# Two sums of squares over partitions: one f32 product each, or two rounded products of a split square

## Chip, cores and metric

One NeuronCore of a Trainium2 chip runs the whole kernel in one launch. The metric is device time in microseconds (us). The engines are TensorE (PE, with its weight loads as PEld), VectorE (DVE), ScalarE (ACT), GpSimd (POOL) and SyncE (SP, which issues most DMAs). Each engine works through its own queue in order.

## What is computed

A decoder layer with two branches on x of 1024 x 1024 (f32). Cut to what matters here:

```
proj = h @ w_in[l]                                   # the large product
o_a = hgrn2_chunked(q, k_in, v, log_f)               # branch A, 4 heads of 128
o_a = rms_norm(o_a, hg_norm_gain) * silu(hg)
o_b = diff_attention(dq, dk, dv, lam)                # branch B, 4 heads of 128
o_b = rms_norm(o_b, diff_norm_gain) * (1 - lam_init) * silu(dg)
y = sigmoid(ma) * (o_a @ w_branch_a) + sigmoid(mb) * (o_b @ w_branch_b)
x = x + gate * rms_norm(y @ w_out, g_post)
```

`rms_norm` divides by the root of the mean of squares over the 128 values of a head. In the kernel a head's outputs lie with those 128 values on the 128 partitions and the 1024 positions along the free dimension, so that the mean is a sum over partitions.

## The kernel before

The input projection is done in rounds of 28 products (four groups of seven, a Strassen scheme: M1, M2, M6, M5, M7, M3, M4). A product is 12 matmuls of 128x128 by 128x512 in the rounded type fp32r (each operand split into a high and a low part; lines 935 to 937), into the PSUM banks `pj`. A half product (six matmuls) is a slot; a round has 56 slots. In front of each slot's six matmuls stand small units of the two branches, placed by tables of slot numbers (`SSA_AT`, `SSB_AT` and so on): in round r the recurrence of head r and, 56 slots later, the attention of head r run beside the products. The time of a unit is thus fixed by its place in PE's queue, and ACT and DVE go through the same slot numbers in order.

Units that matter here, all numbered by slot within a round:
- `ssa` (recurrence slots 61 and 63, which are slots 5 and 7 of the next round) and `ssb` (attention slots 34 and 50): the sum over partitions of the squares of one half (512 positions) of a head's output, a product of the f32 matrix `ones` with the f32 squares. There are 8 of each. `ssa` writes bank `by` and reads `k`; `ssb` writes bank `bx` and reads `sig` or `p1`.
- Ahead of each, DVE clips the outputs (`clip_a`, `clip_b`), ACT squares them in place (lines 1318 and 1325, slots 59, 60 and 31, 46). Behind each, ACT copies the sum out (lines 1247, 1252), DVE takes reciprocals (`over`, line 1698), ACT a root, DVE finishes.
- `qk` (line 751; slots 2, 7, 12, ...) computes two rows of scores into `sp`, and waits until ACT has taken the exponentials of the row before (line 1212; slots 4, 9, ...). `tr` (line 760) transposes them once DVE has combined the two maps (lines 1705 to 1707; slots 6, 11, ...).
- `lev` (lines 792, 794; last one in slot 48) with DVE's updates of `q` and `k` (lines 1618, 1619) and copies into `sc` (1653), and `kt` (line 800, slots 50 and 51), which transposes `k` after the last of them.
- For each product ACT rounds the weights (line 1197, `w_hi`) and POOL takes the remainder (line 624, `w_lo`), two products ahead. DVE adds three of seven products to copies that ACT has taken (line 1599).

In round 4, which has no recurrence, only the attention of head 3 stands beside the products.

Of the kernel before, what the change touches and what calls it, by code (L numbers as in the profile page):

```python
# [6 lines left out]
ALU = mybir.AluOpType  # L7
ACT = mybir.ActivationFunctionType
AX_X = mybir.AxisListType.X
F32 = mybir.dt.float32  # L10
# [99 lines left out]
TR_AT = [(8, 9), (13, 14), (18, 19), (23, 24), (28,), (33,), (37,), (41,)]  # L110
PV_AT = [11, 16, 21, 26, 30, 35, 39, 43]
DVT_AT = (0, 3)
SSB_AT = (34, 50)
CLIPB_AT, SQB_AT, OVERB_AT, ROOTB_AT, FINB_AT = (30, 45), (31, 46), (42, 51), (45, 53), (46, 54)
GATEB_AT, MULB_AT = (10, 13), (11, 14)
F_AT = (10, 13)
LEV_AT = [18, 23, 28, 32, 37, 41, 45, 48]
VT_AT, KT_AT, ST_AT, O_AT, SSA_AT = (21, 26), (50, 51), (53, 54), (56, 57), (61, 63)
CLIPA_AT, SQA_AT, OVERA_AT, ROOTA_AT, FINA_AT = (58, 59), (59, 60), (63, 70), (73, 73), (75, 76)
GATEA_AT, MULA_AT = (25, 28), (26, 29)  # L120
GATEA_0, MULA_0 = (30, 33), (31, 34)
SUM_HIGH_AT = {16: M6, 20: M5, 24: M7, 28: M4}
# [79 lines left out]
def build(nc, x, c, w_ada, b_ada, g_pre, g_post, w_in, lb_logits, hg_norm_gain, lambda_q1, lambda_k1,  # L202
          lambda_q2, lambda_k2, diff_norm_gain, w_branch_a, w_branch_b, w_out, out):
    ctx = ExitStack()
    with ctx:  # L205
# [32 lines left out]
        kt = block_at("kt", 38)  # L238
        sc = block_at("sc", 39)
        v_tok = block_at("v_tok", 40)  # L240
        f2 = block_at("f2", 41, 0.5)
        st = block_at("st", 41)
        rms = block_at("rms", 41)
# [9 lines left out]
        oa = block_at("oa", 52)  # L253
        ob = block_at("ob", 53)
        sig = block_at("sig", 54, 0.5)


        vec_rows = block_at("vec_rows", 52, 1, F32, [P, P])
# [34 lines left out]
        ident = small("ident", P)  # L293
        causal = small("causal", P)
        ones = small("ones", P)
        cols = small("cols", 256)
        masks = [small(f"mask{n}", 64) for n in range(len(LEVELS) - 1)]
        used = [0]
# [82 lines left out]
        s_sqb = sem("s_sqb")  # L381
        s_clipa, s_clipb = sem("s_clipa"), sem("s_clipb")
        s_sqa = sem("s_sqa")
        s_rva, s_rvb = sem("s_rva"), sem("s_rvb")
        s_rta, s_rtb = sem("s_rta"), sem("s_rtb")
        s_oah = sem("s_oah")
# [61 lines left out]
        def y_free(eng, e):  # L448

            eng.wait_ge(s_unit["o"], 2 * HEADS)  # L450
            if e == 4:
                eng.wait_ge(s_unit["dvt"], 2 * HEADS)
            elif e == 5:
                eng.wait_ge(s_unit["ssa"], 2 * HEADS)
            elif e in (3, 7):
                eng.wait_ge(s_oah, 2 * HEADS)
# [272 lines left out]
        def _(pe):  # L729
            def unit(u):  # L730
# [25 lines left out]
                if name == "tr":  # L756
                    i, half = divmod(n, 2)
                    pe.wait_ge(s_comb, row_no(h, i) + 1)
                    for kk in range(4 * half, min(i + 1, 4 * half + 4)):
                        last = pe.transpose(bx[:, (kk % 4) * P:(kk % 4 + 1) * P], p0[i % 2][:, kk * P:(kk + 1) * P],  # L760
                                            ident[:, :])
                elif name == "pv":
                    i = n
                    pe.wait_ge(s_xa, x_act(("tr", h, 2 * i + (i >= 4))) + 1)
                    for kk in range(i + 1):
                        last = pe.matmul(by[:, 0:P], va_tok[:, kk * P:(kk + 1) * P], at[:, kk * P:(kk + 1) * P],  # L766
                                         start=(kk == 0), stop=(kk == i))
                elif name in ("vt", "dvt"):
                    if name == "vt" and h == 0:
                        pe.wait_ge(s_pja, 5 + n)  # L770
                    else:
                        pe.wait_ge(s_pjd, dve_reads(at_product(h, 1 if name == "vt" else 2, M3 if n else M2)))
                    for kk in range(4):
                        cc = 4 * n + kk
                        last = pe.transpose(bx[:, kk * P:(kk + 1) * P], stage[:, cc * P:(cc + 1) * P], ident[:, :])
                elif name == "lev":
                    if n == 0:
                        pe.wait_ge(s_f, 2 * h + 2)
                        pe.wait_ge(s_pja, act_reads(at_product(h, 0, M4)))
                        if h:  # L780
                            pe.wait_ge(s_pjd, dve_reads(at_product(h, 0, M7)))
                    else:
                        pe.wait_ge(s_upd, 8 * h + n)
                    for cc in range(NT):
                        for z in range(2):
                            zs = slice(cc * P + 64 * z, cc * P + 64 * z + 64)
                            zp = slice(64 * z, 64 * z + 64)
                            if n == 0:
                                last = pe.matmul(by[zp, cc * 64:(cc + 1) * 64], k[:, zs], q[:, zs], start=True, stop=True)
                            elif n < 7:  # L790
                                qv = q[:, zs].rearrange("p (b s j) -> p b s j", s=2, j=LEVELS[n - 1])[:, :, 1, :]
                                last = pe.matmul(by[zp, cc * 32:(cc + 1) * 32], k[:, zs], qv, start=True, stop=True)  # L792
                            elif z == 0:
                                last = pe.matmul(by[zp, cc * 64:(cc + 1) * 64], k[:, zs],
                                                 q[:, cc * P + 64:(cc + 1) * P], start=True, stop=True)
                elif name == "kt":
                    pe.wait_ge(s_upd, 8 * h + 8)
                    for kk in range(4):
                        cc = 4 * n + kk
                        last = pe.transpose(by[:, kk * P:(kk + 1) * P], k[:, cc * P:(cc + 1) * P], ident[:, :])  # L800
                elif name == "st":
                    pe.wait_ge(s_ya, y_act(("kt", h, n)) + 1)
                    for cc in range(4 * n, min(4 * n + 4, NT - 1)):
                        cs = slice(cc * P, (cc + 1) * P)
                        last = pe.matmul(by[:, (cc % 4) * P:(cc % 4 + 1) * P], kt[:, cs], v_tok[:, cs], start=True, stop=True)
                elif name == "o":
                    pe.wait_ge(s_yd, y_dve(("st", h, 1)) + 1)
                    for cc in range(4 * n, 4 * n + 4):
                        cs = slice(cc * P, (cc + 1) * P)
                        dst = by[:, (cc % 4) * P:(cc % 4 + 1) * P]  # L810
                        last = pe.matmul(dst, v_tok[:, cs], sc[:, cs], start=True, stop=(cc == 0))
                        if cc > 0:
                            last = pe.matmul(dst, st[:, (cc - 1) * P:cc * P], q[:, cs], start=False, stop=True)
                elif name == "ssa":
                    pe.wait_ge(s_sqa, 2 * h + n + 1)
                    last = pe.matmul(by[:, :], ones[:, :], k[:, n * HALF:(n + 1) * HALF], start=True, stop=True)
                elif name == "ssb":
                    pe.wait_ge(s_sqb, 2 * h + n + 1)
                    last = pe.matmul(bx[:, :], ones[:, :], (sig, p1)[n][:, 0:HALF], start=True, stop=True)
                last.then_inc(s_unit[name], 1)  # L820


# [170 lines left out]
        def _(act):  # L993
# [55 lines left out]
            square(1)  # L1049
            act.wait_ge(s_vec, 1)  # L1050
            act.activation(c_sig, c_col, ACT.Sigmoid).then_inc(s_sigc, 1)
            act.wait_ge(s_lb, 1)
            act.activation(lb, lb_diff, ACT.Sigmoid).then_inc(s_sigc, 1)
            act.activation(one_less_lb, lb_diff, ACT.Sigmoid, scale=-1.0).then_inc(s_sigc, 1)
# [160 lines left out]
            def unit(u):  # L1215
# [12 lines left out]
                    act.activation(ob[:, n * P:(n + 1) * P], by[:, 0:P], ACT.Copy).then_inc(s_ya, 1)  # L1228
                elif name == "vt":
                    act.wait_ge(s_unit["vt"], 2 * h + n + 1)  # L1230
                    act.activation(part(v_tok, n), bx[:, :], ACT.Copy).then_inc(s_xa, 1)
                elif name == "dvt":
                    act.wait_ge(s_unit["dvt"], 2 * h + n + 1)
# [39 lines left out]
            for m in range(2 * PROD, SLOTS + 2):  # L1273
# [42 lines left out]
                for h, e in recurrence(m, SQA_AT):  # L1316
                    act.wait_ge(s_clipa, 2 * h + e + 1)
                    act.activation(part(k, e), part(k, e), ACT.Square, scale=DOWN).then_inc(s_sqa, 1)
                for h, e in recurrence(m, ROOTA_AT):
                    act.wait_ge(s_rva, 2 * h + e + 1)  # L1320
                    act.activation(part(rms, e), part(rms, e), ACT.Sqrt).then_inc(s_rta, 1)
                for h, e in attention(m, SQB_AT):
                    act.wait_ge(s_clipb, 2 * h + e + 1)
                    t = (sig, p1)[e][:, 0:HALF]
                    act.activation(t, t, ACT.Square, scale=DOWN).then_inc(s_sqb, 1)
                if m in SUM_HIGH_AT:
                    e = SUM_HIGH_AT[m]
                    if e == M6:
# [107 lines left out]
        def _(dve):  # L1436
# [110 lines left out]
                dve.tensor_tensor(b_lo[m][:, :], raw[:, :], b_hi[m][:, :].bitcast(F32), ALU.subtract).then_inc(s_blo[m], 1)  # L1547

            dve.wait_ge(s_gain, 1)
            dve.wait_ge(s_sigc, 3)  # L1550
            dve.wait_ge(s_const, N_CONST)

            def event(n):
# [67 lines left out]
            def unit(u):  # L1621
# [42 lines left out]
                elif name == "st":  # L1664
                    dve.wait_ge(s_unit["st"], 2 * h + n + 1)
                    if n == 0:
                        dve.wait_ge(s_upd, 8 * h + 8)
                    else:
                        dve.wait_ge(s_yd, y_dve(("st", h, 0)) + 1)
                    for cc in range(4 * n, min(4 * n + 4, NT - 1)):  # L1670
# [54 lines left out]
            for m in range(2 * PROD, SLOTS + 2):  # L1725
# [15 lines left out]
                        unit(u)  # L1741
                for h, e in recurrence(m, CLIPA_AT):
                    clip_a(h, e)
                for h, e in recurrence(m, OVERA_AT):
                    dve.wait_ge(s_ya, y_act(("ssa", h, e)) + 1)
                    over(part(rms, e), s_rva)
# [199 lines left out]
```

## Time and profile before

| | us |
|---|---|
| median of three runs (887.14 to 893.91) | 888.22 |
| the profiled execution | 888.69 |
| its span in the trace | 886.8 |
| PE busy | 843.5 (95%) |
| DVE busy | 608.5 (69%) |
| ACT busy | 471.7 (53%) |
| POOL busy | 478.4 (54%) |

The profiled execution's own time and its span differ by 1.9 us, which lie around the span. PE's busy time counts overlapped ends of matmuls, so spacing between starts is the better measure of what a matmul costs.

### The profile page before, as it was taken

What the parts mean: (1) busy time and instruction counts of PE and PEld (TensorE: products, weight loads), DVE (VectorE), ACT (ScalarE), POOL (GpSimd) and SP (SyncE); (2) the same over time, 40 slices, a digit from 0 to 9 for tenths busy, and PEclk for the clock granted to TensorE, in tenths of its full rate; (3) what the DMA queues carried; (4) which work ended last, traced back from release to release, by engine and by line L of the source; (5) the groups of instructions that cost most, each with busy time, mean ns of one, the idle gap of its engine ahead of it and who ended that gap; (6) DMA issues with size and microseconds to landing.
All of it is one profiled execution on the core that took longest, in us unless ns stands there. A gap on an engine that the chain in (4) does not pass through costs nothing. (4 is left out here: it accounts for less than half of the span.)

```text
span 886.8 us, 13086 instructions
## 1 busy us (share of the span) xinstructions
PE 843.5 (95%) x4781; PEld 664.3 (75%) x4781; DVE 608.5 (69%) x712; ACT 471.7 (53%) x861; POOL 478.4 (54%) x363
## 2 busy tenths in 40 slices
PE   2899889999999999999999999999999999999997
PEld 2687678777777777777777777777788888887885
DVE  3888984788794888694897866864500166697775
ACT  7676323786443875445865336745455641333453
POOL 6054685455464455554545653566787822236884
PEclk9899899999999999999999999999999999999999
DMA  9914131102101101110120121021211561302222
GB/s 327 342 45 147 50 94 48 49 1 72 49 15 58 48 14 59 49 48 24 48 72 1 49 72 32 17 72 49 71 48 48 180 224 47 95 24 95 96 95 95
DMA packets 75586, 68.11 MB, mean 77 GB/s; under 512 B 3652, under 2 KB 65156, under 8 KB 75524
## 3 DMA queue, kind: packets, MB, share of 16 engines
q1 hardware_dynamic: 75408, 67.25, 23.6%
q8 instruction: 39, 0.64, 0.3%
q14 instruction: 23, 0.19, 0.1%
q10 hardware_dynamic: 116, 0.03, 0.0%
HBM read 58.88 MB, written 8.39 MB: 76 GB/s over the span
## 5 line engine op out<-in xcount | busy, mean ns | idle before, releaser
L624 POOL TENSOR_TENSOR w_lo<-w_raw,w_hi 128x512 fp32r<-128x512 f32 x140 | 193.5, 1384 | 258.7 <-ACT w_hi L1197 257.2
L935 PE MATMUL pj<-b_hi,w_hi 128*128 128x512 f32 x712 | 299.7, 421 | 6.3 <-DVE dk L1599 3.4
L937 PE MATMUL pj<-b_hi,w_lo 128*128 128x512 f32 x712 | 279.6, 393 | 0.0
L936 PE MATMUL pj<-b_lo,w_hi 128*128 128x512 f32 x712 | 279.0, 392 | 0.0
L935 PEld LDWEIGHTS pj<-b_hi,w_hi 128*128 128x128 f32 x712 | 134.4, 189 | 49.3 <-issue 12.5
L937 PEld LDWEIGHTS pj<-b_hi,w_lo 128*128 128x128 f32 x712 | 134.2, 188 | 30.0
L936 PEld LDWEIGHTS pj<-b_lo,w_hi 128*128 128x128 f32 x712 | 134.8, 189 | 25.6 <-issue 3.1
L1197 ACT ACTIVATE w_hi<-w_raw 128x512 fp32r<-128x512 f32 x132 | 82.8, 627 | 63.5 <-PE pj L937 57.4
L605 POOL TENSOR_TENSOR w_raw<-w_raw,w_raw 128x512 f32<-128x512 f32 x66 | 91.2, 1382 | 2.9
L685 POOL TENSOR_TENSOR wb_lo<-wb_raw,wb_hi 128x512 fp32r<-128x512 f32 x16 | 22.7, 1422 | 63.3 <-ACT wb_hi L1267 63.3
L1212 ACT ACTIVATE p<-sp,cols 128x1024 f32<-128x1024 f32 (+7 forms) x64 | 46.9, 738 | 0.8
L702 POOL TENSOR_TENSOR w_lo<-y_all,w_hi 128x512 fp32r<-128x512 f32 x24 | 37.6, 1589 | 15.0 <-ACT w_hi L1363 14.7
L1599 DVE TENSOR_TENSOR y_all<-pj,snap_a 128x512 f32<-128x512 f32 x8 | 5.5, 692 | 58.4 <-PE pj L937 58.4
L1223 ACT ACTIVATE at<-bx 128x512 f32<-128x512 f32 (+3 forms) x48 | 23.3, 485 | 41.6 <-PE bx L760 41.6
L1630 DVE TENSOR_REDUCE cols<-sp 128x2 f32<-128x2048 f32 (+7 forms) x32 | 43.4, 1358 | 1.1
L766 PEld LDWEIGHTS by<-at,va_tok 128*128 128x128 f32 x288 | 36.3, 191 | 10.6 <-issue 8.8
L766 PE MATMUL by<-at,va_tok 128*128 128x128 f32 x288 | 38.0, 277 | 5.1 <-issue 2.9
L1629 DVE TENSOR_TENSOR sp<-sp,causal 128x256 f32<-128x256 f32 x32 | 13.8, 430 | 40.4 <-PE sp L751 40.4
L751 PE MATMUL sp<-dk,dq 64*128 64x512 f32 (+3 forms) x192 | 39.6, 517 | 0.4
L1618 DVE TENSOR_TENSOR q<-q,f 128x512 f32<-128x512 f32 x24 | 24.0, 1000 | 22.7 <-PE by L792 22.7
L1267 ACT ACTIVATE wb_hi<-wb_raw 128x512 fp32r<-128x512 f32 x16 | 10.1, 630 | 52.1 <-PE bx L974 27.0
L605 POOL TENSOR_TENSOR w_sum<-w_raw,w_raw 128x512 f32<-128x512 f32 x22 | 30.0, 1365 | 10.1 <-PE pj L937 8.0
(290 smaller groups left out, 1647.3 us busy)
## 6 DMA issues: line engine op xcount, KB each, us to landing
w_raw<-in_w_in SPq DMA_DIRECT2D x96, 256.0 KB, 4.1
x_in<-in_x SPq DMA_DIRECT2D x8, 512.0 KB, 7.2
ada<-in_w_ada SPq DMA_DIRECT2D x16, 256.0 KB, 7.1
ada<-in_w_ada SPq DMA_DIRECT2D x8, 512.0 KB, 8.0
ada_g<-in_w_ada SPq DMA_DIRECT2D x8, 512.0 KB, 3.9
res<-in_x SPq DMA_DIRECT2D x8, 512.0 KB, 4.4
out_x<-rows_o SPq DMA_DIRECT2D x7, 512.0 KB, 2.9
o_kepta<-oa SPq DMA_DIRECT2D x4, 512.0 KB, 6.0
```

The costliest lines, as they stand in the source:

```text
L605: pool.tensor_tensor(dst[:, :], a[:, :], b[:, :], op).then_inc(s_wsum, 1)
L624: pool.tensor_tensor(w_lo[slot(v)][:, :], raw[:, :], w_hi[slot(v)][:, :].bitcast(F32), ALU.subtract).then_inc(s_wlo, 1)
L702: pool.tensor_tensor(in_four(w_lo[slot(v)][:, :]), raw, in_four(w_hi[slot(v)][:, :].bitcast(F32)), ALU.subtract).then_inc(s_wlo, 1)
L751: last = pe.matmul(sp[:, m, c0:c1_], dq[rows, i * P:(i + 1) * P], dk[rows, c0:c1_], start=True, stop=True)
L766: last = pe.matmul(by[:, 0:P], va_tok[:, kk * P:(kk + 1) * P], at[:, kk * P:(kk + 1) * P], start=(kk == 0), stop=(kk == i))
L935: pe.matmul(bank[:, :], wh, part(bh, kk), start=(fresh and kk == 0), stop=False, skip_group_check=True)
L936: pe.matmul(bank[:, :], wh, part(bl, kk), start=False, stop=False, skip_group_check=True)
L937: last = pe.matmul(bank[:, :], wl, part(bh, kk), start=False, stop=(kk == 3), skip_group_check=True)
L1197: act.activation(w_hi[slot(v)][:, :], raw[:, :], ACT.Copy).then_inc(s_whj, 1)
L1212: act.activation(dst[:, 0:w], sp[:, m, 0:w], ACT.Exp, bias=nm[:, 2 * (i % 2) + m:2 * (i % 2) + m + 1], scale=0.125, accum_out=den[:, 2 * ( ...
L1618: dve.tensor_tensor(qv, qv, pairs[:, :, 0:1].to_broadcast(shape), ALU.mult)
L1630: dve.reduce_max(mx[:, 0:2], sp[:, :, 0:w], AX_X).then_inc(s_max, 1)
```

## The change

Where ACT has squared a half, it now also copies the square into an fp32r tile (`sqa_hi`, `sqb_hi`). DVE subtracts that copy from the square into a second fp32r tile (`sqa_lo`, `sqb_lo`). PE then does two fp32r products with `ones_r`, an fp32r copy of `ones` made once near the start, into one accumulation. The slots of `ssa` go from (61, 63) to (62, 64), the first `ssb` from 34 to 35, and the first `over` behind `ssa` from 63 to 65.

```diff
-SSB_AT = (34, 50)
+SSB_AT = (35, 50)
+SQL_A_AT, SQL_B_AT = (61, 62), (33, 48)
...
-VT_AT, KT_AT, ST_AT, O_AT, SSA_AT = (21, 26), (50, 51), (53, 54), (56, 57), (61, 63)
-CLIPA_AT, SQA_AT, OVERA_AT, ROOTA_AT, FINA_AT = (58, 59), (59, 60), (63, 70), (73, 73), (75, 76)
+VT_AT, KT_AT, ST_AT, O_AT, SSA_AT = (21, 26), (50, 51), (53, 54), (56, 57), (62, 64)
+CLIPA_AT, SQA_AT, OVERA_AT, ROOTA_AT, FINA_AT = (58, 59), (59, 60), (65, 70), (73, 73), (75, 76)
...
# TensorE
-                    pe.wait_ge(s_sqa, 2 * h + n + 1)
-                    last = pe.matmul(by[:, :], ones[:, :], k[:, n * HALF:(n + 1) * HALF], start=True, stop=True)
+                    pe.wait_ge(s_sqal, 2 * h + n + 1)
+                    pe.matmul(by[:, :], ones_r[:, :], part(sqa_hi, n), start=True, stop=False)
+                    last = pe.matmul(by[:, :], ones_r[:, :], part(sqa_lo, n), start=False, stop=True)
                 elif name == "ssb":
-                    pe.wait_ge(s_sqb, 2 * h + n + 1)
-                    last = pe.matmul(bx[:, :], ones[:, :], (sig, p1)[n][:, 0:HALF], start=True, stop=True)
+                    pe.wait_ge(s_sqbl, 2 * h + n + 1)
+                    pe.matmul(bx[:, :], ones_r[:, :], sqb_hi[h][n][:, :], start=True, stop=False)
+                    last = pe.matmul(bx[:, :], ones_r[:, :], sqb_lo[n][:, :], start=False, stop=True)
...
# ScalarE, near the start and behind each square
+            act.wait_ge(s_const, N_CONST)
+            act.activation(ones_r[:, :], ones[:, :], ACT.Copy).then_inc(s_sigc, 1)
...
                     act.activation(part(k, e), part(k, e), ACT.Square, scale=DOWN).then_inc(s_sqa, 1)
+                    act.wait_ge(s_unit["o"], 2 * h + 2)
+                    act.wait_ge(s_sqa, 2 * h + e + 1)
+                    act.activation(part(sqa_hi, e), part(k, e), ACT.Copy).then_inc(s_sqah, 1)
...
                     act.activation(t, t, ACT.Square, scale=DOWN).then_inc(s_sqb, 1)
+                    if e == 0 and h < HEADS - 1:
+                        act.wait_ge(s_oah, 2 * h + 2)
+                    if h == HEADS - 1:
+                        act.wait_ge(s_unit["pv" if e else "o"], (NT if e else 2) * HEADS)
+                    elif e:
+                        act.wait_ge(s_unit["ssb"], 2 * h + 1)
+                    act.wait_ge(s_sqb, 2 * h + e + 1)
+                    act.activation(sqb_hi[h][e][:, :], t, ACT.Copy).then_inc(s_sqbh, 1)
...
# VectorE, behind the units of the slot
+                for h, e in recurrence(m, SQL_A_AT):
+                    dve.wait_ge(s_sqah, 2 * h + e + 1)
+                    dve.tensor_tensor(part(sqa_lo, e), part(k, e), part(sqa_hi, e).bitcast(F32), ALU.subtract).then_inc(s_sqal, 1)
+                for h, e in attention(m, SQL_B_AT):
+                    dve.wait_ge(s_sqbh, 2 * h + e + 1)
+                    dve.tensor_tensor(sqb_lo[e][:, :], (sig, p1)[e][:, 0:HALF], sqb_hi[h][e][:, :].bitcast(F32),
+                                      ALU.subtract).then_inc(s_sqbl, 1)
```

The rest of the diff places the new tiles in memory that other tiles use at other times, adds their semaphores, and adds four waits that keep those uses apart (the copy of `v_tok`, the first of `st`, and two kinds of tiles of `y`).

## Rows read from the trace of the kernel before

**Rows 1.** The page: busy time of PE, and its granted clock by slice.

```profile
PE 843.5 (95%) x4781; PEld 664.3 (75%) x4781; DVE 608.5 (69%) x712; ACT 471.7 (53%) x861; POOL 478.4 (54%) x363
...
PEclk9899899999999999999999999999999999999999
```

**Rows 2.** The source view of the two sums' lines: name, count, duration in ns.

```profile
L816 PE MATMUL by<-k,ones x16: 590/592/697, 160.8 to 546.1; 128*128 128x512 f32 x16
...
L819 PE MATMUL bx<-sig,ones x8: 591/592/592, 229.7 to 601.1; 128*128 128x512 f32 x8
```

**Rows 3.** Timeline of PE around the first ssb: start, duration, instruction.

```profile
229.43 0.40 PE L937 MATMUL pj<-b_hi,w_lo 128*128 128x512 f32 x1
229.66 1.02 PE L819 MATMUL bx<-sig,ones 128*128 128x512 f32 x2
230.12 0.80 PE L935 MATMUL pj<-b_hi,w_hi 128*128 128x512 f32 x1
230.75 0.40 PE L936 MATMUL pj<-b_lo,w_hi 128*128 128x512 f32 x1
```

**Rows 4.** Timeline of PE around the second ssb, slot 50.

```profile
260.71 0.39 PE L937 MATMUL pj<-b_hi,w_lo 128*128 128x512 f32 x1
260.94 1.02 PE L819 MATMUL bx<-p,ones 128*128 128x512 f32 x2
262.38 0.63 PE L800 MATMUL by<-ident,k 128*128 128x128 f32 x4 [0.43 <-DVE sc L1653]
262.77 0.47 PE L935 MATMUL pj<-b_hi,w_hi 128*128 128x512 f32 x1
```

**Rows 5.** Timeline of DVE in the same stretch.

```profile
259.29 1.79 DVE L1618 TENSOR_TENSOR q<-q,cols 128x512 f32<-128x512 f32 x1
261.00 0.68 DVE L1619 TENSOR_TENSOR k<-k,cols 128x512 f32<-128x512 f32 x1
261.61 0.68 DVE L1653 COPY sc<-by 64x512 f32<-64x512 f32 x1
262.21 0.15 DVE L1663 TENSOR_TENSOR cols<-cols 128x8 f32<-128x8 f32 x1
```

**Rows 6.** Timeline of POOL in the same stretch.

```profile
259.11 1.43 POOL L624 TENSOR_TENSOR w_lo<-w_raw,w_hi 128x512 fp32r<-128x512 f32 x1 [2.12 <-ACT w_hi L1197]
262.39 1.29 POOL L624 TENSOR_TENSOR w_lo<-w_raw,w_hi 128x512 fp32r<-128x512 f32 x1 [1.86 <-ACT w_hi L1197]
```

**Rows 7.** Timeline of ACT from the first square of ssa to the exponentials.

```profile
285.83 0.63 ACT L1318 ACTIVATE k<-k 128x512 f32<-128x512 f32 x1 [0.55 <-DVE k L1685]
286.37 0.62 ACT L1197 ACTIVATE w_hi<-w_raw 128x512 fp32r<-128x512 f32 x1
...
290.49 0.20 ACT L1212 ACTIVATION_READ_ACCUMULATOR p<-sp,cols 128x1 f32 x1
```

**Rows 8.** Timeline of ACT, an instruction that waits for the one before it.

```profile
303.28 0.61 ACT L1157 ACTIVATE f<-f 128x512 f32<-128x512 f32 x1
303.93 0.72 ACT L1169 ACTIVATE k<-k,cols 128x512 f32<-128x512 f32 x1
```

**Rows 9.** Timeline of PE in slots 63 and 64.

```profile
290.97 1.77 PE L751 MATMUL sp<-dk,dq 64*128 64x512 f32 x8
...
295.38 0.48 PE L935 MATMUL pj<-b_hi,w_hi 128*128 128x512 f32 x1
```

**Rows 10.** Timeline of PE, behind the second ssb of head 3.

```profile
632.97 0.50 PE L935 MATMUL pj<-b_hi,w_hi 128*128 128x512 f32 x1 [0.61 <-DVE y L1599]
```

**Rows 11.** Timeline of POOL, the last of the constants at the start.

```profile
3.39 4.19 POOL L582 TENSOR_SCALAR_AFFINE_SELECT mask<-mask 128x64 f32<-128x64 f32 x12
```

**Rows 12.** Timeline of PE, its two longest idle times between products.

```profile
97.83 1.92 PE L792 MATMUL by<-q,k 128*64 128x32 f32 x32 [3.01 <-DVE sc L1660]
...
131.53 0.50 PE L935 MATMUL pj<-b_hi,w_hi 128*128 128x512 f32 x1 [1.54 <-DVE dk L1599]
```

**Rows 13.** Busy time by window: PE, PEld, DVE, ACT, POOL, PE's granted clock, DMA.

```profile
98.00:100.00 2.00, 2.00 (x33) 1.94 (x34) 1.96 (x3) 0.00 (x0) 0.63 (x1) 0.50 0.00 0
```

More of the change, by code:

```diff
@@ L240, in build @@
         v_tok = block_at("v_tok", 40)
+        sqa_hi = block_at("sqa_hi", 40, 1, F32R)
+        sqa_lo = block_at("sqa_lo", 37, 1, F32R)
         f2 = block_at("f2", 41, 0.5)
@@ L255, in build @@
         sig = block_at("sig", 54, 0.5)
+        sqb_hi = [[block_at("sqb_hi", 41.5, 0.5, F32R)] * 2] * (HEADS - 1)
+        sqb_hi.append([block_at(f"sqb_hi_last{e}", (39, 50)[e], 0.5, F32R) for e in range(2)])
+        sqb_lo = [block_at("sqb_lo0", 54, 0.5, F32R), block_at("sqb_lo1", 49, 0.5, F32R)]
         vec_rows = block_at("vec_rows", 52, 1, F32, [P, P])
@@ L295, in build @@
         ones = small("ones", P)
+        ones_r = small("ones_r", P, F32R)
         cols = small("cols", 256)
@@ L383, in build @@
         s_sqa = sem("s_sqa")
+        s_sqah, s_sqal = sem("s_sqah"), sem("s_sqal")
+        s_sqbh, s_sqbl = sem("s_sqbh"), sem("s_sqbl")
         s_rva, s_rvb = sem("s_rva"), sem("s_rvb")
@@ L452, in y_free @@
                 eng.wait_ge(s_unit["dvt"], 2 * HEADS)
-            elif e == 5:
+            elif e == 6:
+                eng.wait_ge(s_unit["ssb"], 2 * HEADS - 1)
+            elif e in (2, 5):
                 eng.wait_ge(s_unit["ssa"], 2 * HEADS)
@@ L1230, in unit @@
                     act.wait_ge(s_unit["vt"], 2 * h + n + 1)
+                    if h:
+                        act.wait_ge(s_unit["ssa"], 2 * h)
                     act.activation(part(v_tok, n), bx[:, :], ACT.Copy).then_inc(s_xa, 1)
@@ L1549, in _ @@
             dve.wait_ge(s_gain, 1)
-            dve.wait_ge(s_sigc, 3)
+            dve.wait_ge(s_sigc, 4)
             dve.wait_ge(s_const, N_CONST)
@@ L1667, in unit @@
                         dve.wait_ge(s_upd, 8 * h + 8)
+                        if h:
+                            dve.wait_ge(s_unit["ssb"], 2 * h)
                     else:
```

## Prediction

> **What bounds the kernel now.** I read the page first: PE is busy for 95% of the span at a granted clock near full [rows 1]. So a change to PE's own work shows in the time, as long as PE is never made to wait. Then the list of what PE waits for: between 100 and 640 us it is under a dozen stalls of 0.2 to 1.5 us, nearly all for DVE. The timelines of the four engines around each of the two sums are what decides, since PE's queue is in order: one late operand holds everything behind it. They repeat every 126.4 us, once for each head; I show the second round for ssa and the first attention for ssb.
>
> **What is removed: one f32 product, 16 times.** Each is recorded as two matmuls [rows 2]. Its cost is best read from starts. The ssb begins at 229.66, the second matmul of the next product at 230.75, 1.09 later; two matmuls of a product follow each other by 0.23 (229.43 to 229.66) [rows 3]. So the f32 product takes 1.09 - 0.23 = 0.86 us of PE. **Added:** two fp32r matmuls of the same shape, 2 x 0.23 = 0.46. The gain is 0.40 us each, 16 x 0.40 = 6.4 us if nothing else moved. That is the ceiling.
>
> **What is added on ACT and DVE.** A copy of 128x512 takes 0.62, and an ACT instruction that may overlap the one before it starts 0.54 after it (285.83 to 286.37) [rows 7]. The copy waits for the square itself, so it starts only when the square has ended, as at 303.93, 0.04 after 303.28 + 0.61 [rows 8]. So each copy sets ACT's queue back by 0.63 + 0.04 + 0.53 - 0.54 = 0.66. A subtraction of two 128x512 operands takes 0.68 on DVE when POOL is quiet, but 1.79 when a POOL operation has begun first: the one that starts at 259.29 ends at 261.08, 0.54 after POOL's end at 259.11 + 1.43 = 260.54 [rows 5, 6]. The Trainium skill (Advanced Engine Details and Errata, VectorE Performance Modes) says that VectorE's second port to SBUF is shared with GpSimd and that the two block each other; these rows agree, and the page alone gives no price.
>
> **First ssb of each head, slot 35.** Its clip and square lie at slots 30 and 31, and DVE's queue has 2.5 us idle where the subtraction comes (slot 33). The new place is one half product (1.38) later than 229.66, at 231.04, and the subtraction ends near 230.96. So nothing is late: 4 x -0.40 = -1.6.
>
> **Second ssb of heads 0 to 2, slot 50, the step that I think decides.** Here DVE is the late engine: it works without a pause from 244.85 to 262.36, and PE already waits for it, since `kt` behind the ssb starts only at 262.38, when the copy into `sc` has ended [rows 4, 5]. The old ssb stood in that wait (260.94) and needed nothing new from DVE. The new one needs the subtraction, which the diff puts behind the whole unit of slot 48, that is behind the 0.15 operation at 262.21 [rows 5]. It can start at 262.40 at the earliest. POOL's `w_lo` starts at 262.39 and runs 1.29 [rows 6], and nothing in the change moves it. It is a tie; since DVE has two more waits to pass, I let POOL be first: it ends at 263.68, the subtraction 0.54 later, 264.22, PE's ssb starts 0.09 later (as 262.38 after 262.29), the pair takes 0.46, `kt` 0.39, and the product that started at 262.77 [rows 4] starts at 265.16. That is +2.39 a head. If DVE is first, the subtraction ends at 263.08 and the product starts at 264.02, +1.26. Behind this wait stand `kt`, the products and all else in PE's queue; ACT's copy of the sum comes some 1.7 to 2.8 us later and with it DVE's reciprocal, but DVE idles 1.0 us before the next work that PE sends, so I see nothing more late. Sum: 3 x 2.39 = 7.2 (bounds 3.8 and 7.2). The gain of these three ssb is inside that figure.
>
> **Second ssb of head 3.** No recurrence is beside it, so it isn't late, but 7 us behind it PE waits 0.61 for DVE [rows 10], on a chain (sum, reciprocal, addition) that starts with ACT's work on the product before. What PE saves here it waits there: 0.
>
> **The ssa pair, slots 62 and 64.** The first square (285.83) starts as soon as the clip allows, and ACT is busy without a gap from there until the exponentials end at 290.69 [rows 7]; the `qk` at 290.97 needs them [rows 9]. The copy of 0.66 stands ahead of them, so they end at 291.35, and `qk` starts near 291.47 (in the first round the row is 0.14 behind its exponentials), 0.50 later. From `qk` to the product at 295.38 was 4.41 [rows 9], with one f32 product in it, 0.86; now both fp32r pairs are settled by then, one inside this stretch: 4.41 - 0.86 + 0.46 = 4.01, hence 295.48, +0.1. In the first round `qk` already waited for the exponentials, so it is +0.3. The subtractions are ready before PE comes (287.9 for 288.6, and 294.3 for 295.1). Sum of four heads: +0.6 instead of -3.2. Were the copy hidden, this would be -3.2; were the second subtraction to meet POOL (it leads by under 0.1), +2.4 more.
>
> **Start.** ACT waits for POOL's constants, which end at 7.58 [rows 11], two microseconds before it gets there, and copies 128x128. A copy of four times the width takes 0.62 [rows 7]; I take 0.2, between 0 and 0.6, on the path to the first products.
>
> **Sum.** -1.6 + 7.2 + 0 + 0.6 + 0.2 = +6.4 us. Against the profiled execution's 888.69 that is 895.1; that execution lies 0.5 above the median 888.22, so against the median 894.6. With DVE first at slot 50 it is -1.6 + 3.8 + 0.8 = +3.0, 891.2.
>
> **Rivals.**
> - *The clock drops.* In slot 50 PE would be idle from 260.71 + 0.39 = 261.10 [rows 4] to 264.31, 3.2 us, or 2.1 with DVE first. The trace has one idle time of 3.01 us, and from there on the granted clock is half (1.2 of 2.4 GHz) until about 104.5, and one of 1.54 us behind which matmuls keep their 0.4 us [rows 12, 13]. A drop costs: the `lev` unit 0.8 more (1.92 against 1.12) and the eleven steps to 104.52 2.2 more, 3.0 in all. One to three drops: 897.6 to 903.6, most likely near 900. The Trainium skill (TensorE: Matmul & The Clock Gate, Why this matters for your kernels) warns of idle gaps between bursts of matmuls for this reason. It decides once POOL wins the tie. This is the rival on the slow side.
> - *The gain survives.* If slot 50's subtraction isn't late, because DVE's queue is ahead there or the copy on ACT costs nothing ahead of the exponentials, the sum goes to between -6.4 + 0.2 (882.0) and about -2 (886). Against it speaks that the wait for `sc` at 262.38 recurs at 388.81 and 515.25, with DVE's rows equal to 0.01 us. Even the whole gain is 0.7%.
> - *PE isn't bound by these units at all* (the slack is elsewhere), so that neither gain nor loss shows: 888. Against it: each f32 product visibly pushes the next product back [rows 3].
>
> **Chances.** The stall at slot 50 with the clock kept: 0.48 (894.6 by the tie as I took it, 891.2 the other way); with one drop or more 0.35; the gain survives 0.13; nothing moves 0.04. The likeliest case gives 894.6. The range leaves out the ceiling of the gain and the last bit of three drops: 886 to 903. One per cent, 8.9 us, is about what a measurement of this kernel can tell from no change; faster than 879.3 is beyond the ceiling, 0.02; slower than 897.1 needs the clock to drop, 0.33; within, 0.65.
>
> **What the profile after would show.** PE's two matmuls of the sum about 0.23 apart, and 0.86 shrunk to 0.46 at the first ssb. At the second ssb of three heads an idle time of PE of 2 to 3 us ended by DVE's `sqb_lo`, and that subtraction at 0.7 or 1.8 us with POOL's `w_lo` beside it. `qk` of slot 63 released by ACT's exponentials. A granted clock of 0.5 near 261, 388 or 515 us if it drops. I am wrong if PE finds `sqb_lo` ready at slot 50, if ACT's copy doesn't move the exponentials, or if PE's waits elsewhere shrink by what is added here.

## The result, and the profile after

The changed kernel is slower, by 1.3%. Its median is 902.13 us (899.74 to 904.00, 4 runs) against 890.92 us (887.14 to 893.91, 4 runs) for the kernel before; the ratio is 1.0131 with a 95% interval of 1.0099 to 1.0164. The forecast was 894.6 us with a range of 886 to 903; it was +6.4 us on a median of 888.22, and the measured ratio makes +11.6 of it. The profiled execution took 903.66 us with a span of 901.7 us, 14.9 more than the span before.

The list of what PE waits for, of the changed kernel (engine, line, what it waited for: us in total, times, longest):

```profile
PE bx L831 <- DVE sqb_lo L1779: 9.7, 3, 3.2
...
PE sp L762 <- ACT p L1227: 4.1, 4, 1.2
...
PE pj L948 <- DVE dq L1627: 3.0, 1, 3.0
```

The first two of these lines are not in the list of before at all; the third was 0.8 there. The timeline of slot 50 in the first attention, all engines by start, which answers to [rows 4 to 6]:

```profile
263.37 0.39 PE L950 MATMUL pj<-b_hi,w_lo 128*128 128x512 f32 x1
...
264.89 0.14 DVE L1691 TENSOR_TENSOR cols<-cols 128x8 f32<-128x8 f32 x1
265.05 1.26 POOL L635 TENSOR_TENSOR w_lo<-w_raw,w_hi 128x512 fp32r<-128x512 f32 x1 [1.23 <-ACT w_hi L1212]
265.07 1.79 DVE L1779 TENSOR_TENSOR sqb_lo<-p,sqb_hi 128x512 fp32r<-128x512 f32 x1
...
267.00 0.76 PE L831 MATMUL bx<-sqb_hi,ones_r 128*128 128x512 f32 x1 [3.25 <-DVE sqb_lo L1779]
267.57 0.63 PE L832 MATMUL bx<-sqb_lo,ones_r 128*128 128x512 f32 x1
...
267.99 1.05 PE L811 MATMUL by<-ident,k 128*128 128x128 f32 x4
...
268.70 0.78 PE L948 MATMUL pj<-b_hi,w_hi 128*128 128x512 f32 x1
```

POOL begins 0.02 us ahead of DVE, the subtraction takes 1.79, and PE stands for 3.25 us. Behind that wait matmuls that took 0.39 take 0.63 to 0.78. The granted clock in windows of 2 us behind the three waits (start:end, length, busy time of PE, PEld, DVE, ACT, POOL, then the clock as a share of 2.4 GHz, DMA):

```profile
266.00:268.00 2.00, 1.00 (x3) 0.73 (x4) 0.86 (x1) 0.00 (x0) 1.99 (x2) 0.64 0.24 68
268.00:270.00 2.00, 2.00 (x8) 1.81 (x7) 1.14 (x1) 1.19 (x2) 0.00 (x0) 0.51 1.07 304
...
396.00:398.00 2.00, 0.94 (x2) 0.72 (x3) 0.92 (x1) 0.00 (x0) 2.00 (x2) 0.56 0.17 45
398.00:400.00 2.00, 2.00 (x8) 1.75 (x7) 1.08 (x1) 1.19 (x2) 0.05 (x1) 0.50 1.04 302
...
530.00:532.00 2.00, 2.00 (x6) 1.51 (x6) 2.00 (x1) 0.56 (x1) 0.00 (x0) 0.50 0.91 266
```

The columns 0.50 and 0.51 are 1.2 of 2.4 GHz. The clock drops behind each of the three.

The first ssb, which answers to [rows 3], and the exponentials with the `qk` that needs them, which answer to [rows 7, 9]:

```profile
233.19 0.69 DVE L1779 TENSOR_TENSOR sqb_lo<-sig,sqb_hi 128x512 fp32r<-128x512 f32 x1
...
233.71 0.39 PE L950 MATMUL pj<-b_hi,w_lo 128*128 128x512 f32 x1
234.03 0.47 PE L831 MATMUL bx<-sqb_hi,ones_r 128*128 128x512 f32 x1
234.34 0.40 PE L832 MATMUL bx<-sqb_lo,ones_r 128*128 128x512 f32 x1
234.57 0.61 PE L777 MATMUL by<-at,va_tok 128*128 128x128 f32 x4
...
292.32 0.63 ACT L1335 ACTIVATE k<-k 128x512 f32<-128x512 f32 x1 [0.52 <-DVE k L1715]
293.04 0.63 ACT L1338 ACTIVATE sqa_hi<-k 128x512 fp32r<-128x512 f32 x1
293.58 0.62 ACT L1212 ACTIVATE w_hi<-w_raw 128x512 fp32r<-128x512 f32 x1
...
298.05 1.77 PE L762 MATMUL sp<-dk,dq 64*128 64x512 f32 x8 [0.96 <-ACT p L1227]
```

From the product's last matmul to the unit behind the pair it is 234.57 - 233.71 = 0.86; three steps of 0.23 would be 0.69. The pair had to wait a little: the subtraction ends at 233.19 + 0.69 = 233.88, the pair starts 0.15 behind it, and the step behind that start is 0.31 and not 0.23. It is the same 0.15 in the first three heads. In head 3 the subtraction was done 2.5 us ahead (614.34 + 0.77 = 615.11), and there the steps are 0.23, 0.22 and 0.23:

```profile
617.38 0.39 PE L950 MATMUL pj<-b_hi,w_lo 128*128 128x512 f32 x1
617.61 0.39 PE L831 MATMUL bx<-sqb_hi_last,ones_r 128*128 128x512 f32 x1
617.83 0.39 PE L832 MATMUL bx<-sqb_lo,ones_r 128*128 128x512 f32 x1
618.06 0.83 PE L777 MATMUL by<-at,va_tok 128*128 128x128 f32 x6
```

At the first square of ssa the copy puts `w_hi` 1.26 behind the square (293.58 - 292.32), where it was 0.54 behind it [rows 7]. So the queue goes back by 0.72.

To see where 14.9 us went I took matching PE rows of both timelines and subtracted their starts. The lag of the changed kernel is 0.4 at its 97 us, 2.6 at 134, 2.7 ahead of the first slot 50 and 6.5 behind it; 6.3 and 11.6 around the second, 11.4 and 15.4 around the third, 14.7 behind head 3. That is 3.8 + 5.3 + 4.0 = 13.1 us at the three slots 50; 0.3, 0.1, 0.1 and 0.1 at the four heads' ssa; -0.25, -0.25, -0.27 and -0.40 at the four first ssb; -0.40 at the second ssb of head 3; and 2.2 between 98 and 134 us, where no operation of the change lies (the lone wait for `dq`; see the last two experiments).

### The profile page after: what moved, and what is told of

Same layout as the page of the kernel before. It is cut to its first block and busy times, and to the rows that moved or that the text cites. A ratio compares the mean times of both kernels' runs of the same rounds, so it can differ in the third digit from the quotient of the medians.

```text
span 901.7 us, 13145 instructions
## 1 busy us (share of the span) xinstructions
PE 841.3 (93%) x4781; PEld 666.6 (74%) x4781; DVE 621.8 (69%) x728; ACT 481.0 (53%) x878; POOL 481.2 (53%) x363
## 5 line engine op out<-in xcount | busy, mean ns | idle before, releaser
L948 PE MATMUL pj<-b_hi,w_hi 128*128 128x512 f32 x712 | 296.6, 417 | 8.5 <-DVE dk L1627 3.2
L948 PEld LDWEIGHTS pj<-b_hi,w_hi 128*128 128x128 f32 x712 | 135.4, 190 | 51.4 <-issue 13.1
L616 POOL TENSOR_TENSOR w_raw<-w_raw,w_raw 128x512 f32<-128x512 f32 x66 | 95.1, 1441 | 3.6 <-DMA w_raw<-in_w_in 0.7
L713 POOL TENSOR_TENSOR w_lo<-y_all,w_hi 128x512 fp32r<-128x512 f32 x24 | 38.7, 1632 | 15.0 <-ACT w_hi L1391 14.7
```

The costliest lines, as they stand in the source:

```text
L616: pool.tensor_tensor(dst[:, :], a[:, :], b[:, :], op).then_inc(s_wsum, 1)
L713: pool.tensor_tensor(in_four(w_lo[slot(v)][:, :]), raw, in_four(w_hi[slot(v)][:, :].bitcast(F32)), ALU.subtract).then_inc(s_wlo, 1)
L948: pe.matmul(bank[:, :], wh, part(bh, kk), start=(fresh and kk == 0), stop=False, skip_group_check=True)
```

## The experiments

Twelve runs follow, two of them repeats, in four groups, each group beside runs of the kernel before on the same chip. Where a kernel was timed, the ratio to the kernel before is given with its 95% interval.

**1. The second ssb alone as it was.** The second ssb of each head is the f32 product again, without its copy and its subtraction; the other 12 pairs stay.

```diff
-pe.matmul(bx, ones_r, sqb_hi[h][n], start=True, stop=False)
-pe.matmul(bx, ones_r, sqb_lo[n], start=False, stop=True)
+pe.matmul(bx, ones, p1[:, 0:HALF], start=True, stop=True)   # n == 1, waits for s_sqb
```

> The change with the second ssb of each head as before: one f32 product in slot 50, no copy and no subtraction for it; all else as changed. Theory (the subtraction in front of slot 50 is late three times, and with its clock drops costs 13.1 of the 14.9 us of span): the three stalls of 3.25 us are gone, PE waits 0.43 for the copy into sc as before, and the time is near 889, ratio to before 0.995 to 1.003. Rival (the added load on ScalarE and VectorE costs it wherever it stands): 4 of 16 copies and subtractions fewer give back a quarter, about 898. Rival (the difference is only where the clock happens to drop): no stall moves, 900.

Measured: 889.56 us beside 889.55, ratio 0.9997 (0.9975 to 1.0018). The whole loss is gone. So it lies at slot 50, and the other 12 pairs together are worth nothing that can be measured.

**2. The subtraction one slot earlier.** All 16 pairs; DVE takes the second remainder in slot 47, ahead of the last two updates of the recurrence.

```diff
-SQL_A_AT, SQL_B_AT = (61, 62), (33, 48)
+SQL_A_AT, SQL_B_AT = (61, 62), (33, 47)
```

> The change with the subtraction of the second ssb one slot earlier in VectorE's queue (47 for 48), ahead of the unit of the last level. Theory: the same work on VectorE, but in front of the wait for sc and not behind it: ssb finds its operand, kt waits 0.6 longer than before, PE's longest idle time there is about 1.5, the clock holds, and the time is near 891 to 892. Rival (load, not place): 902, as the full change. If GpSimd's operation gets in front of it, up to 1.3 a head more, 895.

Measured: 889.75 us, ratio 0.9997 (0.9978 to 1.0016). PE finds `sqb_lo` ready and waits at `kt` instead, 1.45 where it was 0.43 [rows 4]. The timeline of this kernel:

```profile
258.77 0.68 DVE L1779 TENSOR_TENSOR sqb_lo<-p,sqb_hi 128x512 fp32r<-128x512 f32 x1
259.37 1.78 DVE L1646 TENSOR_TENSOR q<-q,cols 128x512 f32<-128x512 f32 x1
...
262.45 0.63 PE L811 MATMUL by<-ident,k 128*128 128x128 f32 x4 [1.45 <-DVE sc L1681]
262.83 0.47 PE L948 MATMUL pj<-b_hi,w_hi 128*128 128x512 f32 x1
```

The pair has been done inside this wait, as the old product was. So it is hardly the work of the change that costs; it is its place in DVE's queue. The subtraction still delays the updates behind it: in this profile the products start 0.6 later at each of the three slots 50, where the changed kernel had 3.8 to 5.3.

**3. The ssb one slot later.** PE comes to it in slot 51, and the reciprocal behind it moves from slot 51 to 52.

```diff
-SSB_AT = (35, 50)
+SSB_AT = (35, 51)
-... OVERB_AT, ... = ..., (42, 51), ...
+... OVERB_AT, ... = ..., (42, 52), ...
```

> The change with the second ssb one slot later on PE (51 for 50, and the reciprocal behind it in 52 for 51); the subtraction stays behind the last level. Theory: kt is released by sc at once as before, the product of slot 50 covers the subtraction, and ssb meets it ready; the reciprocal starts 2 us later than before, and st in slot 54 may wait up to 0.7. Time 890 to 893. Rival (load, not place): 902.

Measured: 899.54 us, ratio 1.0112 (1.0081 to 1.0143), a miss of 7 us. The wait for `sqb_lo` is gone, but the list of waits has a new place, and the timeline shows what stands there:

```profile
PE by L816 <- issue: 8.0, 4, 2.6
```

```profile
268.09 3.34 DVE L1728 RECIPROCAL sig<-sig 128x512 f32<-128x512 f32 x1
...
272.08 0.28 DVE L1703 COPY st<-by 128x128 f32<-128x128 f32 x1
...
273.61 0.91 PE L816 MATMUL by<-v_tok,kt 128*128 128x128 f32 x6 [2.59 <-issue]
```

The reciprocal (3.34) now stands ahead of DVE's copies out of `by`, for which PE's next `st` waits. My own move of the reciprocal made stalls of 2.57 to 2.59 in three heads, where those of 3.25 had been removed; behind the third of them the clock is at half (about 532.5 to 535.5 us), and PE waits once, near 653 us, for POOL's `w_lo` (2.3).

**4. Filled wait.** Twelve unread fp32r matmuls into `bx` ahead of the wait, at the second ssb of heads 0 to 2. They only keep PE at work.

```diff
+if n == 1 and h < HEADS - 1:
+    for z in range(12):
+        pe.matmul(bx, ones_r, part(b_hi[M1], z % 4), start=True, stop=True)
 pe.wait_ge(s_sqbl, 2 * h + n + 1)
```

> The change with twelve matmuls that nobody reads put into the wait in front of the second ssb of heads 0 to 2 (same bank, overwritten by the sum; the output is unchanged). They fill 2.8 of the 3.25 us. Theory (of the 13.1 us at slot 50, 7.2 are the wait and 5.9 the half clock behind it): the wait ends at the same time, no granted clock under 1 there, and the time is 6 less than the full change, near 896. Rival (the clock drops whatever PE does there, or costs nothing): 902 or more.

Measured: 894.21 us, ratio 1.0050 (1.0031 to 1.0069). The subtraction is as late as in the changed kernel (POOL first again, by 0.02), but the clock stays. The timeline, then a window behind the same place of the second head:

```profile
260.09 0.39 PE L953 MATMUL pj<-b_hi,w_lo 128*128 128x512 f32 x1
...
260.31 2.88 PE L832 MATMUL bx<-b_hi,ones_r 128*128 128x512 f32 x12
...
261.77 1.29 POOL L635 TENSOR_TENSOR w_lo<-w_raw,w_hi 128x512 fp32r<-128x512 f32 x1 [1.23 <-ACT w_hi L1215]
261.79 1.81 DVE L1782 TENSOR_TENSOR sqb_lo<-p,sqb_hi 128x512 fp32r<-128x512 f32 x1
...
263.66 0.50 PE L834 MATMUL bx<-sqb_hi,ones_r 128*128 128x512 f32 x1 [0.47 <-DVE sqb_lo L1782]
...
264.58 0.47 PE L951 MATMUL pj<-b_hi,w_hi 128*128 128x512 f32 x1
```

```profile
394.00:396.00 2.00, 2.00 (x13) 1.65 (x12) 2.00 (x1) 0.82 (x2) 0.00 (x0) 1.00 0.95 276
```

This row gives the pure price of the late operand. From the last matmul of slot 49 to the first of slot 50 it is 264.58 - 260.09 = 4.49, and it was 262.77 - 260.71 = 2.06 [rows 4]: +2.43 a head. The prediction had +2.39. In this kernel's profile the lag grows by 2.44 at each of the three, and the clock is full behind all three. The rest of what the changed kernel loses at these slots, 13.1 - 3 x 2.4 = 5.9 us, goes with PE's idleness: twelve useless products save it.

**5. The copies over a behind the exponentials.** The second ssb is f32; both copies of `sqa_hi` stand in slot 60 behind the exponentials, and the subtractions, ssa and the reciprocal move with them.

```diff
-SSA_AT = (62, 64); SQL_A_AT = (61, 62); OVERA_AT = (65, 70)
+SSA_AT = (64, 66); SQL_A_AT = (62, 62); OVERA_AT = (66, 70)
```

> The second ssb as before (f32), and for ssa both copies on ScalarE behind the exponentials of slot 60, both subtractions in slot 62, the two sums in slots 64 and 66 and the first reciprocal in 66. Theory (the copy ahead of the exponentials moves qk and eats the gain of ssa): PE's four waits for p of 1.0 to 1.2 us are gone, and against the run with the second ssb as f32 (889.6) this is 4.1 less, less some 0.3 for the later places: 885 to 886.5, ratio to before 0.995 to 0.997. Rival (qk waits for something else, or the two subtractions in a row on VectorE delay the scores' maxima and tr): no gain, 889 to 891.

Measured: 895.05 us, ratio 1.0058 (1.0035 to 1.0081), a miss of 9 us. The wait for the exponentials shrinks only from 4.1 to 3.1, since PE comes to `qk` earlier when no ssa stands ahead of it, and there is a new one, 4.2 in four times, for the copy of the second sum. The timeline:

```profile
304.08 1.01 ACT L1231 ACTIVATE p<-sp,cols 128x896 f32<-128x896 f32 x1
...
306.58 0.59 ACT L1268 ACTIVATE rms<-by 128x512 f32<-128x512 f32 x1
...
307.22 2.05 PE L777 MATMUL by<-at,va_tok 128*128 128x128 f32 x16 [1.04 <-ACT rms L1268]
```

At slot 66 the sum comes behind the next row's exponentials (slot 65) in ACT's queue, and the bank `by` stays taken. I had looked at the exponentials in front of the copies and not at those behind the sums. In the profile the four heads' ssa cost 1.2 to 1.4 us each, 4.9 in all. That is not the whole miss there: another 4.8 us lie between 98 and 134 us, where PE waits 2.96 for `dq` and the clock is then at half until about 125 us (see experiment 11). This profiled execution, 897.48, was the longest of the eight.

**6. One copy alone.** The kernel before, with only the first copy of each head's squares over a, unread: four ACT instructions more.

```diff
 act.activation(part(k, e), part(k, e), ACT.Square, scale=DOWN).then_inc(s_sqa, 1)
+if e == 0: act.activation(part(sqa_hi, e), part(k, e), ACT.Copy).then_inc(s_sqah, 1)
```

> The kernel before with one thing added: the copy of the first square of ssa into an fp32r tile that nobody reads, at its place ahead of the exponentials (4 copies). Both sums stay f32 products and the output is unchanged. Theory: qk in slot 63 starts 0.5 to 0.7 us later in each of four rounds, with a wait for p that the kernel before doesn't have, and the time is 2 to 2.7 us more than before. Rival (the copy is hidden): 0.

Measured: 893.75 us, ratio 1.0034 (1.0016 to 1.0052), that is +3.0. `qk` waits for the exponentials 0.75, 0.53, 0.51 and 0.52, 2.3 in all, and the lag grows by 2.5 at the four places; this profile also has 2.1 more between 98 and 134 us, so that a part of the 3.0 may be that. So the copy costs about as much as the pairs over a give back (8 x 0.40 = 3.2 at the most).

**7. Both moved.** Experiments 2 and 5 together, all 16 pairs.

> All 16 sums as two fp32r products, with both remedies: the second ssb's subtraction in slot 47, and ssa as in the run with the late copies. Theory: against the run with only the subtraction moved (889.8) the four waits for p go: 885.5 to 887, ratio to before 0.996 to 0.998. Rival: 890 or more.

Measured: 895.13 us, ratio 1.0067 (1.0047 to 1.0088), a miss for both reasons found in 5: the waits for `rms` are 4.2 again, and its profile too has 4.8 us more between 98 and 134 us.

**8. The changed kernel once more**, for its profile.

> The changed kernel once more, for its trace. Three waits of 3.2 us or, where VectorE wins the tie with GpSimd, 2.1 us at slot 50; and in the first round (88 to 134 us) the wait for dq is 0.8 us as in the kernel before, if the 2.96 us of the first trace was where the clock happened to drop, or 3 us again, if the change brings it.

Measured: 901.13 us, one run. At slot 50 PE waits 3.25, 2.12 and 3.25. In the second head DVE was first, by 0.02, as the timeline shows:

```profile
395.15 0.69 DVE L1779 TENSOR_TENSOR sqb_lo<-p,sqb_hi 128x512 fp32r<-128x512 f32 x1
395.17 1.81 POOL L635 TENSOR_TENSOR w_lo<-w_raw,w_hi 128x512 fp32r<-128x512 f32 x1 [1.27 <-ACT w_hi L1212]
```

The same two instructions, in the other order: 0.69 and 1.81 instead of 1.79 and 1.26. The order isn't fixed by the program; it changes from head to head and from run to run.

**9. Only the first ssb.** Four pairs, at slot 35; everything else as before.

> Only the first sum over b of each head (slot 35) is a pair; the two sums over a and the second over b are the f32 product of the kernel before, in their old slots. It leaves out nothing. By the offsets of the changed kernel's profile each first pair gives back 0.20 to 0.27 us, four of them 1.0, and the added copy of the ones at the start may cost 0.2 to 0.4: 0.6 to 0.8 us below the kernel before, which five rounds will hardly tell from nothing; a ratio of 0.997 to 1.001. PE should wait at slot 50 only for sc (0.43) and not for the exponentials ahead of qk. Rival: the full 0.40 of each, 1.6 us, 0.998. Against both: a ratio above 1.003 would say that something that I have not seen, such as the wait for dq near 116 us (0.8 or 2.96), comes with the new instructions at the start.

Measured: 887.15 us beside 889.04, ratio 0.9983 (0.9962 to 1.0004). This is the lowest median here, but its interval still reaches 1. In its profile the four pairs give back 0.27, 0.25, 0.26 and 0.40, 1.2 us.

**10. The sums over a in f32.** The changed kernel without its eight pairs over a.

```diff
-SSA_AT = (62, 64); OVERA_AT = (65, 70)
+SSA_AT = (61, 63); OVERA_AT = (63, 70)
```

> The changed kernel with the sums over a (slots 61 and 63) as f32 products again; both sums over b stay pairs, the second with its subtraction at slot 48. My reading is that the eight pairs over a are worth about nothing (prediction +0.6; the offsets of the changed kernel's profile give +0.3, +0.1, +0.1 and -0.7), so this kernel should lose what the changed one loses: 11 to 13 us over the kernel before, ratio 1.011 to 1.014, with the wait for sqb_lo of 3.2 at three slots and half clock behind it, and no wait for the exponentials. Rival: the copies ahead of the exponentials cost what they cost alone (3.0), more than the pairs give back; then this kernel is 2 to 3 us faster than the changed one, 1.009 to 1.011.

Measured: 894.02 us, ratio 1.0064 (1.0041 to 1.0087), where my reading wanted 1.011 to 1.014 and the rival 1.009 to 1.011. The profile shows another cause: DVE was first at all three slots 50, by 0.01 to 0.02. The timeline, and the windows behind the three waits:

```profile
262.63 0.69 DVE L1772 TENSOR_TENSOR sqb_lo<-p,sqb_hi 128x512 fp32r<-128x512 f32 x1
262.64 1.82 POOL L635 TENSOR_TENSOR w_lo<-w_raw,w_hi 128x512 fp32r<-128x512 f32 x1 [1.27 <-ACT w_hi L1211]
...
263.46 0.47 PE L830 MATMUL bx<-sqb_hi,ones_r 128*128 128x512 f32 x1 [2.12 <-DVE sqb_lo L1772]
```

```profile
264.00:266.00 2.00, 2.00 (x13) 1.69 (x12) 1.17 (x1) 1.09 (x2) 1.71 (x2) 1.00 0.11 31
...
392.00:394.00 2.00, 2.00 (x6) 1.54 (x6) 1.67 (x1) 0.79 (x2) 1.20 (x1) 0.50 0.38 104
...
522.00:524.00 2.00, 2.00 (x13) 1.65 (x12) 2.00 (x1) 0.60 (x1) 0.28 (x1) 1.00 0.88 253
```

The waits are 2.12, and the clock drops behind one of three instead of behind three of three. With the eight pairs gone, the phase of the two engines had moved by a few hundredths, and that was enough.

**11. The kernel before once more**, for the stretch of 98 to 134 us.

> The kernel before once more, for its profile between 98 and 134 us. Two forms of this stretch have been seen: PE at half clock near 98 to 104 us and then a wait for dq of 0.8 (before, and three experiments), or the clock back early and then a wait for dq of 2.96 with half clock behind it, some 2 us more (the changed kernel and four others). If the form is chance, this run may show either; if it shows the long wait, the change has no part in it. A time of 887 to 894.

Measured: 886.62 us, one run, with the short wait for `dq` (0.93). The long one (2.96) is in the profiles of the changed kernel, of 5 to 8 (which shared a chip), and the short one in all others. Experiment 6 has it too, and up to that point that kernel does what the kernel before does. So the change has no part in it; what sets it I can't say. By the lags it adds 2.1 to 2.2 us to a profile, and 4.8 in experiments 5 and 7, where the clock stays at half longer.

**12. The tie made certain.** The changed kernel whole; only the subtraction of slot 48 stands ahead of the small product that ends the unit, not behind it.

```diff
                         ins.then_inc(s_yd, 1)
+                        if g == 64:
+                            while due: low_b(*due.pop(0))     # the subtraction
                         pairs = fs[g].rearrange("p (b s) -> p b s", s=2)
                         then(dve.tensor_tensor(fs[2 * g], pairs[:, :, 0], pairs[:, :, 1], ALU.mult))
```

> The changed kernel whole, all 16 pairs in their slots; only DVE's subtraction of slot 48 stands ahead of the product on 128x8 (0.14) that ends that slot's unit, instead of behind it, so that it begins some 0.17 earlier and clearly ahead of POOL's w_lo (in the changed kernel POOL began first, by 0.02). It leaves out nothing. If who begins first on the shared port decides, the subtraction takes 0.69 instead of 1.79, PE's wait at slot 50 goes from 3.25 to about 1.95 in all three heads, 3.9 us less together, and with part of the half clock behind it kept off, the time is 893 to 898, a ratio of 1.005 to 1.009. Where the wait is 2.12 the clock kept up at two slots of three in the kernel with the sums over a in f32, and fell at the one that I saw in the changed kernel. Rival: the loss is in the number of pairs or in the phase of other work, and the ratio stays at 1.013; or POOL's subtraction, now at 1.8 us, makes w_lo late for PE and the wait comes back there.

Measured: 894.78 us, ratio 1.0072 (1.0049 to 1.0095), 5 us less than the changed kernel by the ratios (1.0131 - 1.0072 = 0.0059, of which the intervals leave some 1.5 to 9 us). By the lags in the profiles the three slots 50, taken alone, cost 5.1 us here, 13.1 in the changed kernel and 10.8 in its second profile. The timeline:

```profile
262.35 0.67 DVE L1746 TENSOR_TENSOR sqb_lo<-p,sqb_hi 128x512 fp32r<-128x512 f32 x1
262.50 1.66 POOL L635 TENSOR_TENSOR w_lo<-w_raw,w_hi 128x512 fp32r<-128x512 f32 x1 [1.23 <-ACT w_hi L1212]
262.95 1.23 DVE L1694 TENSOR_TENSOR cols<-cols 128x8 f32<-128x8 f32 x1
263.17 0.47 PE L831 MATMUL bx<-sqb_hi,ones_r 128*128 128x512 f32 x1 [1.96 <-DVE sqb_lo L1746]
```

The waits are 1.96, 1.95 and 1.95, and the clock is at half behind the second only. With all pairs in place, the order of two instructions that begin within 0.2 us of each other is worth about 5 us. The small product pays instead (1.23 for 0.14), and nobody waits for that. Beside experiment 10, which had the same order by luck, the eight pairs over a cost 0.0008, 0.7 us, within the interval of nothing.

## Why the prediction came out as it did

The measured 902.13 lies inside the range, but the case on which the forecast of 894.6 stood (slot 50 stalls, the clock is kept, 0.48) did not happen. The rival on the slow side did, "The clock drops", at 0.35 and 897.6 to 903.6. With it the kernel is slower by more than 1%, to which I had given 0.33, against 0.65 for no change. By the steps:

- *Slot 50, "the step that I think decides"*: shown. 2.43 a head with the clock kept (experiment 4) against 2.39; POOL first in all three heads of the profile, as I had taken the tie, though that was luck: the same program has DVE first in one head of three in experiment 8; undoing this step alone brings the time back to 889.6 (1).
- *The clock*: this is the step that failed. The sum had 0 for it. It is 5.9 us in the profile: 1.4, 2.9 and 1.6 by head, the largest near the 3.0 that I worked out for a drop [rows 12, 13]. My trace had the warning: its idle times of 3.01 and 1.54 us stand on the two sides [rows 12], and I expected 3.2. An idle time that reaches the one that had the drop behind it belonged into the sum, not beside it. The Trainium skill (TensorE: Matmul & The Clock Gate, Why this matters for your kernels) warned of idle gaps, and the runs agree for the long ones: half clock behind all five waits of 3.25, and behind none that was filled. The shorter ones had it sometimes: one of three of 2.59 in experiment 3, one of three of 2.12 in 10 and the one in 8, one of three of 1.95 in 12.
- *First ssb, -0.40 each*: right in head 3 (-0.40), too large in the others (-0.25, -0.25, -0.27). "Nothing is late" was the error: my own times had the subtraction end at 230.96 and PE come at 231.04, 0.08 apart, and PE starts 0.15 behind such an end. At slot 50 I had reckoned 0.09 for this, here nothing. With the late start and the slow step behind it the pair costs 0.86 - 0.23 = 0.63 and not 0.46.
- *The ssa pairs, +0.6*: +0.3, +0.1, +0.1 and +0.1, by the mechanism named; the copy set ACT back by 0.72 (I had 0.66), and one copy alone costs 3.0 (6). Experiment 1 has them within its interval of nothing.
- *Second ssb of head 3, 0*: wrong, it was -0.40. PE again waits 0.61 for `y` [rows 10], but the lag shrinks from 15.13 to 14.73 at this ssb and stays so behind that wait. So what PE waits for came earlier too.
- *Start, +0.2*: not settled. The lag is 0.4 at 88 us and the copy took 0.29, but the kernel before, run again, comes there 2.1 us earlier than its first profile.
- *Not in the sum*: 2.2 us between 98 and 134 us in the profiled execution, which other kernels have too. It belongs to no step.

By the ratios, on a base of 889 us: the full change loses 11.6 us; with the waits filled 4.4; with the tie turned 6.4; with the subtraction in another slot 0. Of the 16 x 0.40 = 6.4 us that PE was to save, four first ssb give 1.2 us, the second ssb of head 3 gives 0.4, those of the other heads nothing, since the old product stood in a wait anyway, and the ssa nothing, since the copy costs what they save.

What stays open: why the clock drops behind the second head's wait of 2.12 or 1.95 and not behind the first and third; what sets which of the two forms the stretch of 98 to 134 us takes; and whether four pairs alone are a real gain (0.9983, interval to 1.0004).

## What to carry to other kernels

A product that stands in a wait for another engine is free, and its replacement must not ask that late engine for anything: look at the queue of the engine that feeds the operand, not at the cost of the matmul. An operand that is ready less than 0.1 us ahead of its reader is late as well: here it cost about 0.15 of each 0.40 to be gained. When a new stall on PE is as long as one that in the same trace has half clock behind it, put the clock into the sum. When a DVE operation and a POOL operation become ready within a few hundredths of a microsecond, make the order certain by moving one of them past a small instruction, and choose the one that PE waits for as the first.

## What the runs showed of the hardware

- Two operations with two operands of 128x512 each, one on DVE and one on POOL, that overlap don't share the time (DVE's subtraction and POOL's `w_lo`): the first to begin keeps its own (DVE 0.69, or POOL 1.26), the second is held until about its end (1.79, or 1.81). A lead of 0.01 to 0.02 us decides, and with it 1.1 us of a PE wait. DVE's reciprocal, with one operand, takes 3.35 beside such operations of POOL and leaves them their 1.29 and 1.28 (kernel before, 262.84).
- A small operation is held as well: 128x8 took 1.23 in place of 0.14 while POOL was at its 128x512.
- Twelve products that nobody reads, 2.75 us of PE's queue in each of three places, made the kernel about 7 us faster than the same kernel that waited idly (1.0050 against 1.0131).
- PE starts a product 0.14 to 0.15 us behind the end of the DVE operation that it waits for (266.86 to 267.00, 233.88 to 234.03), and the next step, at the full clock, is then 0.31 and not 0.23.
